# Two of the four attention heads of each unit normalized on GpSimd instead of VectorE, with statistics in three buffers

## The reference: what is computed

```python
def sink_softmax(score_list, sink):
    s_sink = sink.astype(jnp.float32).reshape(SWA_KV_HEADS, SWA_GROUP, 1, 1)
    m = s_sink
    for sc in score_list:
        m = jnp.maximum(m, jnp.max(sc, axis=-1, keepdims=True))
    ps = [jnp.exp(sc - m) for sc in score_list]
    den = jnp.exp(s_sink - m)
    for p in ps:
        den = den + jnp.sum(p, axis=-1, keepdims=True)
    return [p / den for p in ps]

# latent tokens; context tokens do the same over their own 128 keys
s_ctx = jnp.einsum('bnqhgd,bkhd->bnhgqk', qb, ckf) * scale
s_band = jnp.einsum('bnqhgd,bnkhd->bnhgqk', qb, kw) * scale
s_band = jnp.where(mask[None, :, None, None], s_band, -jnp.inf)
p_ctx, p_band = sink_softmax([s_ctx, s_band], sink)
o = jnp.einsum('bnhgqk,bkhd->bnqhgd', p_ctx, cvf) + jnp.einsum('bnhgqk,bnkhd->bnqhgd', p_band, vw)
```

## Time and profile before

| | |
|---|---|
| median of 3 runs | 3094.34 us (3085.29 to 3094.74) |
| the profiled execution, its own time | 3094.9 us |
| its span, first to last instruction | 3093.1 us |
| busy PE / DVE / ACT / POOL | 93% / 62% / 52% / 9% |
| mean granted TensorE clock | 0.966 of full speed |

### The profile page before, as it was taken

How to read it: one execution, slowest core, us unless ns; L and a number is a source line. 1 busy time by engine, 2 the same in 40 slices (tenths; PEclk the granted TensorE clock), 3 DMA queues, 4 the chain that set the end, 5 groups by cost and what they waited for, 6 DMA issues and landing times.

```text
span 3093.1 us, 38261 instructions
## 1 busy us (share of the span) xinstructions
PE 2890.8 (93%) x14197; PEld 2118.4 (68%) x14197; DVE 1929.6 (62%) x2042; ACT 1605.6 (52%) x1936; POOL 280.8 (9%) x182
## 2 busy tenths in 40 slices
PE   5899998899899999999999996899999999999993
PEld 2698646789657878787887874566666666666662
DVE  2335653435784444444445455788888888888884
ACT  3236423433474334343433342677777777777773
POOL 0000010000002000000000001112111121121111
PEclk7999999999999999999999998999999999999997
DMA  9622464122043222222234238999999999999994
GB/s 383 241 70 69 155 249 162 59 76 66 27 164 112 82 74 93 68 98 68 98 128 154 81 126 328 390 405 401 384 388 391 389 379 383 389 388 379 390 390 177
DMA packets 144391, 684.67 MB, mean 221 GB/s; under 512 B 13940, under 2 KB 14020, under 8 KB 78524
## 3 DMA queue, kind: packets, MB, share of 16 engines
q1 hardware_dynamic: 130832, 613.45, 52.0%
q0 software_dynamic: 11408, 69.78, 7.0%
q10 hardware_dynamic: 2064, 0.26, 0.1%
HBM read 651.91 MB, written 31.60 MB: 221 GB/s over the span
## 4 chain that ended last, share of the span: by engine, by line
PE 86%; DVE 6%; DMA 4%; ACT 2%; issue 1%; POOL 0%; SPq 0%; DVEq 0%; ACTq 0%; POOLq 0%
PE ps L783 36%; PE ps L1220 21%; PE ps L1247 11%; PE ps L802 5%; PE ps L809 3%; PE ps L723 1%; DMA ring<-w_mod 1%; PE ps L1193 1%; DMA hT<-w_exp_gate 1%; PE ps L913 1%; DVE ar L1823 1%; PE ps L746 1%; PE ps L1072 1%; DVE soft L1825 1%; PE ps L1157 1%
## 5 line engine op out<-in xcount | busy, mean ns | idle before, releaser
L783 PE MATMUL ps<-split_weights,split_tokens 128*128 128x512 f32 x5040 | 1164.0, 392 | 20.7 <-DVE ar L1871 8.0
L783 PEld LDWEIGHTS ps<-split_weights,split_tokens 128*128 128x128 f32 x5040 | 951.2, 189 | 231.4 <-issue 15.7
L429 DVE TENSOR_TENSOR split_weights<-ring,split_weights 128x512 fp32r<-128x512 f32 x384 | 267.1, 696 | 731.6 <-ACT split_tokens L426 721.7
L1220 PE MATMUL ps<-split_experts,split_xsT 128*80 128x512 f32 x3072 | 712.8, 393 | 10.7 <-DVE split_experts L1966 10.7
L425 ACT ACTIVATE split_weights<-ring 128x512 fp32r<-128x512 f32 x384 | 242.7, 632 | 778.4 <-PE ps L783 658.6
L1220 PEld LDWEIGHTS ps<-split_experts,split_xsT 128*80 128x80 f32 x3072 | 455.8, 149 | 265.8 <-DVE split_experts L1966 13.9
L1966 DVE TENSOR_TENSOR split_experts<-hT,split_experts 128x2048 fp32r<-128x2048 f32 x240 | 548.1, 2289 | 84.0 <-ACT split_experts L1542 84.0
L1542 ACT ACTIVATE split_experts<-hT 128x2048 fp32r<-128x2048 f32 x240 | 460.8, 1920 | 159.7 <-PE ps L1220 107.1
L1247 PE MATMUL ps<-split_experts,split_hidT 128*80 128x512 f32 x1536 | 360.9, 394 | 0.0
L1247 PEld LDWEIGHTS ps<-split_experts,split_hidT 128*80 128x80 f32 x1536 | 225.5, 148 | 121.8
L432 DVE TENSOR_TENSOR split_tokens<-hT,split_tokens 128x640 fp32r<-128x640 f32 x304 | 249.9, 822 | 0.0
(11 more groups left out here) (256 smaller groups left out, 1952.1 us busy)
## 6 DMA issues: line engine op xcount, KB each, us to landing
ring<-w_mod SPq DMA_DIRECT2D x96, 1024.0 KB, 5.9
hT<-w_exp_gate SPq DMA_DIRECT2D x80, 1024.0 KB, 7.4
hT<-w_exp_up SPq DMA_DIRECT2D x80, 1024.0 KB, 7.3
hT<-w_exp_down SPq DMA_DIRECT2D x80, 1024.0 KB, 9.5
ring<-w_in SPq DMA_DIRECT2D x64, 1024.0 KB, 5.2
ring<-w_exp_gate SPq DMA_DIRECT2D x32, 1024.0 KB, 7.9
ring<-w_exp_up SPq DMA_DIRECT2D x32, 1024.0 KB, 10.3
ring<-w_exp_down SPq DMA_DIRECT2D x32, 1024.0 KB, 7.6
```

Source lines behind the costliest of these rows:

```text
L429: a = self.eng.tensor_tensor(spW[:, s, 1, :], raw, spW[:, s, 0, :].bitcast(F32), ALU.subtract)
L783: mm = pe.matmul(ps[:, b, :], spX[:, s, x, b * P:(b + 1) * P], spW[:, s, w, :], start=(k == 0 and x == w), stop=(k == n_k - 1 and x == 1))
L1220: mm = pe.matmul(ps[0:CAP, bank + i, :], xsT[:, x, k, :], spE[:, s, w, col:col + BANK], start=(k == 0 and x == w), stop=(k == KT - 1 and x ...
```

## The change

In `softmax_back` DVE multiplies heads 0 and 1 only. Heads 2 and 3 are multiplied by GpSimd, which waits for the reciprocal. `sc_n` now counts two for each unit (the reciprocal, and DVE's second product), and the transposes of PE wait for `sc_n` and for GpSimd's counter `pool_step`. `soft` has three buffers instead of two. GpSimd's count in the experts starts 40 higher.

```diff
-        soft = sb("soft", [P, 2, 5, GRP])
+        soft = sb("soft", [P, 3, 5, GRP])
...
+        pool_n = 2 * len(units)
...
             pool.dma_start(T["nv"][0, 0].rearrange("s h d -> s (h d)"), svr[:, NT - 1, :]).then_inc(kv_st, 16)
+
+            for u, (t, g) in enumerate(units):
+                nk = len(unit_keys(t)[1]) * P
+                sf = soft[:, u % 3]
+                pool.wait_ge(sc_n, 2 * u + 1)
+                for j in (2, 3):
+                    p = Sbuf[u % 3][:, j * BANK:j * BANK + nk]
+                    pool.tensor_scalar(p, p, sf[:, 4, j:j + 1], None, ALU.mult).then_inc(pool_step, 1)
             mod_part(2)
...
-                pool.wait_ge(pool_step, e + 1)
+                pool.wait_ge(pool_step, e + (pool_n + 1))
...
                     if i == 0:
-                        pe.wait_ge(sc_n, u + 1)
+                        pe.wait_ge(sc_n, 2 * u + 2)
+                        pe.wait_ge(pool_step, 2 * u + 2)
...
-                sf = soft[:, u % 2]
+                sf = soft[:, u % 3]
...
                 ch.step(dve.tensor_tensor(sf[:, 2, :], sf[:, 2, :], sf[:, 3, :], ALU.add))
-                ch.step(dve.reciprocal(sf[:, 4, :], sf[:, 2, :]))
-                for j in range(GRP):
+                dve.reciprocal(sf[:, 4, :], sf[:, 2, :]).then_inc(sc_n, 1)
+                dve.wait_ge(sc_n, 2 * u + 1)
+                for j in range(GRP // 2):
                     s = Sbuf[u % 3][:, j * BANK:j * BANK + nk]
                     a = dve.tensor_scalar(s, s, sf[:, 4, j:j + 1], None, ALU.mult)
                 a.then_inc(sc_n, 1)
```

More of the change, by code:

```diff
@@ L349, in build @@
         gf_ld, y_sto = sem("gfinal_loaded"), sem("y_out")
+        units = [(t, g) for pair in (0, 2) for t in range(NT) for g in (pair, pair + 1)]
         act_step, dve_step, dve2_step, pool_step = sem("act_step"), sem("dve_step"), sem("dve_loop_step"), sem("pool_step")
+        pool_n = 2 * len(units)
         loads_issued = sem("loads_issued")
@@ L365, in out_pieces @@
             sp.pieces(P_OUT, n * KT, G_OUT, n, mT_last, max(lo, 12), hi)
-        units = [(t, g) for pair in (0, 2) for t in range(NT) for g in (pair, pair + 1)]
         def unit_keys(t):
```

2 lines of the change are left out of this document (1 added, 1 removed).

## The result

| | before | after |
|---|---|---|
| median (7 runs each) | 3092.0 us (3085.29 to 3094.74) | 3102.6 us (3097.19 to 3107.51) |
| ratio after / before | | 1.0041, 95% interval 1.003 to 1.0051 |
| profiled execution, its own time / span | 3094.9 / 3093.1 us | 3097.19 / 3095.0 us |

A forecast was written before the change was run, and what follows sets the result against it. DVE's list was taken to bound the attention stage's first units, a two-unit loop through DVE and PE most later ones. Later units +6.6 to 12.2, first -0.8 to +0.5, less slack 1 to 2: +8 on 3094.9, 3103 us; range 3089 to 3112.

The forecast's parts named there:

- loop A: Attention stage, DVE's own instruction list: 9.03 us a unit in the first units, 6.98 at later four-block units.
- loop B: Attention stage, two-unit loop through DVE's front, reciprocal and multiplications and PE's transposes and scores: 14.49 us at four blocks.
- So the time from the reciprocal to PE's first transpose becomes 0.1 + 2 x 1.49 = 3.1: Four-block units: PE's transposes wait for two GpSimd multiplications, 3.1 us instead of 1.77, up to 4.0.
- With width as the measure: GpSimd's multiplication time scales with columns: 1.49 us for 512, 1.12 for 384, 0.37 for 128.
- The later units: Attention units from unit 4 on: the later GpSimd result lengthens them by 6.6 to 12.2 us together.
- slack: Some units' transposes did not wait for the probabilities, so delays use that up first: 1 to 2 us taken off.
- The first units: Attention units 1 to 3: DVE's shorter list against the longer path through PE, -0.8 to +0.5 us together.
- It decides once PE's wait passes some 2.4 us: PE's transposes start at its lower clock after waits for probabilities above some 2.4 us, costing 1.6 us each time.
- GpSimd is quick: Rival, chance 0.22: a GpSimd multiplication takes 0.8 us or less without waiting for DVE; -2 to -4 us, about 3092.
- Port and clock: Rival, chance 0.17: GpSimd and DVE multiplications exclude one another, +12, and PE's slow starts add 5; 3112 us.
- sign of exclusion: GpSimd's first multiplication of a pair 0.4 to 0.9 us longer than its second, or DVE's second over 1 us.
- DVE gains all: Rival, chance 0.03: PE is not held by GpSimd and 0.79 us a unit shows throughout; some -5 us, 3090.

The follow-up runs named there:

- Experiment 3: Kernel before, with heads 2 and 3 multiplied by nobody and nothing on GpSimd; 0.9984 of the kernel before, 3086.48 us.
- Experiment 8: Changed kernel, with GpSimd multiplying its two heads only in units 0 to 3 and DVE all four from unit 4 on; 1.0015 of the kernel before.
- experiment 5: Changed kernel, with GpSimd also waiting for DVE's second multiplication so the two never multiply together; 1.0066 of the kernel before.
- experiment 7: Changed kernel, with GpSimd multiplying two spare tiles ahead of its two heads in each unit; 1.0145 of the kernel before.
- experiment 4: Changed kernel, with DVE multiplying all four heads, GpSimd two spare tiles, and PE not waiting for GpSimd; 1.0034 of the kernel before.
- experiment 10: Kernel before, with two of the three steps of the last four rotations moved from DVE to GpSimd; 1.0006 of the kernel before.
- experiment 11: Kernel before, with two steps of the last four rotations on GpSimd, its sum held until DVE's multiplications are over; 0.9966, 3083.57 us.
- 9 (second kernel): Kernel before, with PE's filler work moved ahead of each unit's first transposes; 1.0005 of the kernel before.
- experiment 2: Kernel before, with only the third buffer of statistics (soft) added; 1.0004 of the kernel before.
- experiment 6: Changed kernel, with only head 3 on GpSimd and three heads on DVE; 1.0000 of the kernel before.

## Why the prediction was right, and where it was not

**The time and the sign.** Forecast 3103.0, measured 3102.6, inside the range of 3089 to 3112. Against the kernel before the forecast was +8 and the measured difference is 10.6 (ratio 1.003 to 1.0051). The forecast thus lay just within 0.3%, and the result just beyond it. The likeliest case by my chances was "within 0.3%" (0.65); what came was the other (0.32). That the two times agree to 0.4 us is luck: the forecast stood on one execution of 3094.9 us, where the median of seven came to 3092.0, and this offset of 2.9 made up for a difference forecast 2.6 too small. The second measurement of the change was 3106.8, 14.2 over before.

**Which loop bounds what: held.** Experiment 3 shows loop A in the first units and loop B in the later ones: with half of the multiplications gone the first units win 4.6 us (2.9 of them by DVE's list) and the later ones 1.6. Experiment 8 shows that the change's loss in the later units arises there, and experiments 5 and 7 that the time of GpSimd's result sets it.

**"So the time from the reciprocal to PE's first transpose becomes 0.1 + 2 x 1.49 = 3.1": the step on 512 columns held, between the bounds of 3.1 and 4.0.** It is 3.50 + 0.1. Alone, a pair takes 3.10, so a multiplication is 1.55 where the row of 2 partitions said 1.49: the height of the tile does not matter, 4% apart. The company of DVE adds 0.30, within the 0.88 allowed.

**"With width as the measure": failed.** The rule gave 1.12 and 0.37 us for 384 and 128 columns. Undisturbed they take 1.23 and 0.59, with DVE beside them 1.35 and 0.65. Between 512 and 128 columns that is 0.96 us for 384 columns, 2.5 ns each, and 0.27 us that does not shrink. So GpSimd was busy for 53.8 us and not 45: half of the difference is this rule, since the undisturbed instructions of experiment 5 sum to 49.2, and half is DVE's company. One-block units lose too.

**The later units: +7.4 measured, against 6.6 to 12.2 less 1 to 2 of slack.** The four-block loop came to 16.29 us for two units where the bounds gave 14.49 + 1.3 to 2.2 = 15.8 to 16.7. With the measured pairs the way from the reciprocal to the transposes is 3.60, 2.89 and 1.48 us at four, three and one blocks, where 1.77, 1.47 and 0.93 stood; half of each difference over 5, 6 and 4 units is 4.6 + 4.3 + 1.1 = 9.9 us. 7.4 arrived, so slack took 2.5 and not 1 to 2. Too short a GpSimd term and too little slack partly cancelled.

**The first units: -0.8 to +0.5 forecast; +0.7, +5.6 and (experiment 8) +3.0 in three profiles.** The forecast counted units 1 to 3; from the transposes of unit 0 to those of unit 4 the three profiles have +0.1, +3.2 and +1.5. The rest lies ahead of unit 0's transposes, which wait for GpSimd as well (+0.7, +1.6, +1.6), and behind unit 4's. A term was missing here, and it stood in my rival alone: PE's clock. Before, too, three of the five transposes started at the lower level, but two of them on a path that is DVE's: they came at 813.52, 822.43, 831.46, 840.50 and 849.53, some 9.0 apart whether slow or not. (Only the third, at 849.53, was paid: PE works without a pause from there to unit 5's transposes, 8.41 us later, against 6.83 in experiment 3.) In the change PE is in the loop of the first units, so a slow start can be paid there too, 2.6 us for the one at 828.09. With it the stage's excess is 8.1 us in one profile and 13.0 in the other, and the medians of the two sessions differ by 10.6 and 14.2. That slow starts are also what spreads the other runs is inferred: only two runs of the change have a profile.

**"It decides once PE's wait passes some 2.4 us": not so.** After 2.42 us idle PE started at full speed (835.33, above), and after 2.17 us the kernel before started slowly (1.97 at 822.43), as it did in the earlier trace rows after 2.42. After 3.00 there was a start in between (1.54); those after 3.34, 4.36 and 4.50 were slow, while one after 2.76 in experiment 4 was at full speed (838.38, 1.09). The wait's length alone does not tell it.

**The rivals.** *GpSimd is quick* is out: 1.55, not 0.8. *Port and clock* was half right. Its clock part came, in the first units only (experiments 5 and 7 have it in the later ones). Its port part came at 0.30 for GpSimd and 0.44 for DVE at 512 columns. The Trainium skill ("SBUF — State Buffer", Who interferes with whom) says that a DVE float32 TENSOR_SCALAR and a GpSimd operation exclude each other for a whole instruction. The trace does not agree for this pair of operations: by that rule the DVE multiplications of experiment 4 would have stood behind a GpSimd multiplication of 1.55 us, and they lost 0.78. It nearly agrees in experiment 10, where GpSimd ran a TENSOR_TENSOR: DVE lost 1.92 of 2.5. Neither sign of exclusion that I had named came in the change: at 893.75 GpSimd's first multiplication was 0.30 us longer than its second (1.86 and 1.56), and DVE's second took 0.92. *DVE gains all* is out, although experiments 3 and 11 show that the gain existed.

**What I said the profile would show.** 40 instructions of L1850 at 14 us: 40, but 21.5 (10.5 + 8.6 + 2.4); undisturbed, in experiment 5, they sum to 15.0, so 6.5 is the port's part. L604 at 1.5, 1.1 and 0.4: 1.71, 1.35 and 0.65. Stage about 151: 150.0, and 154.9 in the second profile. PE's wait from 0.8 to some 2 at every second four-block unit: 2.50 and 2.17. Put down to POOL: once; the rest under "issue". DVE waiting for scores in the first units: yes, by 0.38, 0.66 and 0.19 us (units 2, 4 and 6).

**Where the expected gain of the idea went.** DVE gave up 14.1 us of work. Of that 7.4 came back (21.5 against 14.1), 6.5 of it by the port. At most 6.2 us could reach the stage's end, 1.6 of them through PE's clock (experiment 3). GpSimd's latency costs more than that, because PE used to have its product 1.77 us after the reciprocal and now has it after 3.60.

**Open.** Why the part ahead of the stage, with the same code, was short (794.7 to 797) in the profiles of most kernels with GpSimd work and of experiment 10, 798.2 to 798.4 in experiments 3, 9 (second kernel) and 11, and long (800 to 801) in those of before and of experiments 2 and 6. The runs show that a profiled run with a short part lay below its kernel's median, so chance is possible; it was not tried by itself. That the loss of the change in the later units is GpSimd's latency does not hang on it, since they are timed by themselves; how much of the 10.6 and 14.2 us is the stage's 8.1 and 13.0, and how much chance in the parts around it, is not shown.

## What to carry to other kernels

Before work is moved to a slower engine, ask how soon its result is wanted and not only how busy the giver is: a loop that passes through the result pays the slower engine's latency even if the busy engine is relieved, and the move pays only for work that nobody waits for soon. Then look at what the giver does at that moment: the same two GpSimd steps gained nothing beside DVE's multiplications in SBUF (1.0006), and 9.8 us when held back to stand beside its operation that reads PSUM (0.9966). A wait put on PE can cost its clock as well, so look at the granted clock before you put a longer stretch down to the loop. And try the limit first: a kernel that leaves the work out (0.9984 here) shows in one run that the best outcome is not worth much.

## What the runs showed of the hardware that was not expected

- GpSimd's TENSOR_SCALAR on 128 rows of float32 took 1.55, 1.23 and 0.59 us at 512, 384 and 128 columns when DVE left it alone, and its TENSOR_TENSOR on 512 columns took only 1.27: the operation with two inputs is the quicker one.
- The Trainium skill ("GPSIMD Engine Reference", Elementwise side-by-side cycle accounting) has 769 ns for 512 elements in a tight loop; the trace does not agree for this TENSOR_SCALAR, whose 1.55 us is twice that.
- DVE's four multiplications of 512 columns took 1.67 us alone, 2.45 beside GpSimd's TENSOR_SCALAR and 3.59 beside its TENSOR_TENSOR. DVE's operation with one input from PSUM and one from SBUF, and its maximum over SBUF, kept their 2.29 us beside the same TENSOR_TENSOR.
- PE may start at its lower level after 2.17 us without work and at full speed after 2.42 in another execution; the same program's first units differed by 4.9 us through this. The lower level can also set in one group behind the start: in experiment 5 the transposes of unit 6 took 1.06 us and the products right behind them 1.76.
